# GpSimd sums the squares of tiles 0 to 3 of each norm, and a norm's first unit takes its high-part products first

## What is computed

```python
def rmsnorm(x, gain):
    xf = x.astype(jnp.float32)
    y = xf * lax.rsqrt(jnp.mean(xf * xf, axis=-1, keepdims=True) + EPS)
    return (y * gain.astype(jnp.float32)).astype(x.dtype)
...
        h = rmsnorm(x, norm1_g[i]) * (1.0 + sc1) + sh1
...
        x = x + g1 * y
        h = rmsnorm(x, norm2_g[i]) * (1.0 + sc2) + sh2
        x = x + g2 * swiglu(h, w_gate[i], w_up[i], w_down[i])
```

## Time and profile before

| | us |
|---|---|
| median of 3 runs (lowest to highest) | 1093.34 (1092.65 to 1093.69) |
| the profiled execution | 1092.77 |
| its span | 1091.0 |

### The profile page before, as it was taken

How to read it: one execution, slowest core, us unless ns; L and a number is a source line. 1 busy time by engine, 2 the same in 40 slices (tenths; PEclk the granted TensorE clock), 3 DMA queues, 4 the chain that set the end, 5 groups by cost and what they waited for, 6 DMA issues and landing times.

```text
span 1091.0 us, 19815 instructions
## 1 busy us (share of the span) xinstructions
PE 1020.5 (94%) x7643; PEld 968.2 (89%) x7643; DVE 784.0 (72%) x1108; ACT 505.5 (46%) x773; POOL 12.8 (1%) x27
## 2 busy tenths in 40 slices
PE   4699889999999989999999999998998999999997
PEld 4696568999999988977899999998887989999997
DVE  5876884898769867675489876986774579876432
ACT  3435743544442354535454443234866553443433
POOL 3000000000000000000000000001000000000000
PEclk9996759999999979999999999997999889999998
DMA  9980458499748948263249974887502429974500
GB/s 303 353 305 4 154 195 268 143 362 317 273 166 318 342 150 319 78 232 117 78 139 362 316 274 163 318 318 255 190 1 77 157 79 355 359 248 157 200 29 39
DMA packets 144413, 232.18 MB, mean 213 GB/s; under 512 B 6249, under 2 KB 75409, under 8 KB 144353
## 3 DMA queue, kind: packets, MB, share of 16 engines
q1 hardware_dynamic: 142993, 228.75, 60.8%
q0 software_dynamic: 1072, 2.05, 0.8%
q10 hardware_dynamic: 288, 0.54, 0.2%
HBM read 230.27 MB, written 1.05 MB: 212 GB/s over the span
## 4 chain that ended last, share of the span: by engine, by line
PE 82%; DVE 7%; ACT 4%; issue 3%; DMA 2%; SPq 1%; DVEq 0%; ACTq 0%
PE M L1425 22%; PE M L1426 22%; PE M L1427 22%; PE AUX L1914 3%; PE AUX L1535 3%; DVE ACC L936 2%; DMA RAW<-in_ada_w 1%; DVE WL L913 1%; ACT WH L565 1%; DMA RAW<-in_wqkv_a 1%; PE AUX L1758 1%; PE AUX L1543 1%; PE M L1702 1%; DVE TMP L993 1%; PE M L1701 1%
## 5 line engine op out<-in xcount | busy, mean ns | idle before, releaser
L1425 PE MATMUL M<-XH,WH 128*128 128x256 f32 x1520 | 441.5, 290 | 13.1 <-DVE XL L998 11.9
L1426 PE MATMUL M<-XL,WH 128*128 128x256 f32 x1520 | 436.2, 287 | 0.0
L1427 PE MATMUL M<-XH,WL 128*128 128x256 f32 x1520 | 435.7, 287 | 0.0
L913 DVE TENSOR_TENSOR WL<-RAW,WH 128x2048 fp32r<-128x2048 f32 x136 | 308.4, 2286 | 84.1 <-ACT WH L565 84.0
L565 ACT ACTIVATE WH<-RAW 128x2048 fp32r<-128x2048 f32 x136 | 258.6, 1914 | 230.4 <-PE M L1427 155.9
L1425 PEld LDWEIGHTS M<-XH,WH 128*128 128x128 f32 x1520 | 298.3, 196 | 16.4 <-issue 14.6
L1426 PEld LDWEIGHTS M<-XL,WH 128*128 128x128 f32 x1520 | 298.3, 196 | 0.2
L1427 PEld LDWEIGHTS M<-XH,WL 128*128 128x128 f32 x1520 | 297.9, 196 | 0.0
L936 DVE SCALAR_TENSOR_TENSOR ACC<-ADA,COND,ACC 128x512 f32<-128x512 f32 x266 | 199.9, 751 | 9.7 <-DMA ADA<-in_ada_w 0.6
L1425 PE MATMUL M<-MH,WH 128*128 (+1 forms) x528 | 150.6, 285 | 0.6 <-DVE TMP L1013 0.6
L1427 PE MATMUL M<-MH,WL 128*128 (+1 forms) x528 | 149.4, 283 | 0.0
(11 more groups left out here) (236 smaller groups left out, 971.4 us busy)
## 6 DMA issues: line engine op xcount, KB each, us to landing
ADA<-in_ada_w SPq DMA_DIRECT2D x68, 1024.0 KB, 6.4
RAW<-in_w_gate SPq DMA_DIRECT2D x44, 512.0 KB, 6.7
RAW<-in_w_up SPq DMA_DIRECT2D x44, 512.0 KB, 7.7
RAW<-in_w_down SPq DMA_DIRECT2D x44, 512.0 KB, 6.1
RAW<-in_w_ffn_in SPq DMA_DIRECT2D x44, 512.0 KB, 6.1
RAW<-in_wqkv_b SPq DMA_DIRECT2D x24, 512.0 KB, 6.2
RAW<-in_w_ffn_out SPq DMA_DIRECT2D x22, 512.0 KB, 4.3
RAW<-in_w_in SPq DMA_DIRECT2D x16, 512.0 KB, 5.7
```

Of the source, the lines that this page charges most:

```text
L913: dve.tensor_tensor(WL[:, s, :], RAW[:, s, :], WH[:, s, :], ALU.subtract).then_inc(l_ready, 1)
L1425: pe.matmul(out_ap, wh, xh, start=start, stop=False, skip_group_check=True)
L1426: pe.matmul(out_ap, wh, xl, start=False, stop=False, skip_group_check=True)
L1427: return pe.matmul(out_ap, wl, xh, start=False, stop=stop, skip_group_check=True)
```

## The change

- **Means.** There is a new tile SQS (128 x 256, fp32) and a new list on GpSimd, `square_sum(n)`: it adds the squares of tiles 0 and 1 into SQS, then tile 2, then tile 3, each as its square is ready, and counts `sq_sum`. Before it overwrites SQS it waits for the means of the norm before (`ssq_ready`). Norms 0 to 4 stand ahead of the seven loads for the mixer in GpSimd's list, norms 5 and 6 behind them.
- TensorE no longer takes the means of tiles 0 to 3: `early_means` and the places in the last `down_unit` go. After the last unit it takes those of tiles 4 and 5, waits for `sq_sum`, takes one of SQS, then those of tiles 6 and 7.
- **High parts first.** In the first unit after norms 1 to 5, TensorE waits for XH of an input tile, takes WH by XH and WL by XH for the four output tiles, then waits for XL of it and takes WH by XL. The products are the same. Norm 0's first unit has a loop of its own and stays.

```diff
+            def square_sum(n):
+
+                if n >= 1:
+                    pool.wait_ge(ssq_ready, n)
+                pool.wait_ge(sq_ready, KT * n + 2)
+                pool.tensor_tensor(SQS[:, :], TMP[:, 0, :], TMP[:, 1, :], ALU.add).then_inc(sq_sum, 1)
+                for j in range(2, 4):
+                    pool.wait_ge(sq_ready, KT * n + j + 1)
+                    pool.wait_ge(sq_sum, 3 * n + j - 1)
+                    pool.tensor_tensor(SQS[:, :], SQS[:, :], TMP[:, j, :], ALU.add).then_inc(sq_sum, 1)
+
+            for n in range(5):
+                square_sum(n)
             pool.wait_ge(w_used, U0["w_in"])
...
+            for n in range(5, 7):
+                square_sum(n)
...
+                if by_rows is not None and not last:
+                    for q, kt in enumerate(kts):
+                        xh, xl = x_of(kt)
+                        pe.wait_ge(hh_ready, KT * by_rows + kt + 1)
+                        for n, (tau, col) in enumerate(taus):
+                            cols = slice(q * width + col, q * width + col + P)
+                            pe.matmul(M[:, tau, :], WH[:, s, cols], xh, start=first and q == 0 and tau % 2 == 0, stop=False,
+                                      skip_group_check=True)
+                            pe.matmul(M[:, tau, :], WL[:, s, cols], xh, start=False, stop=False, skip_group_check=True)
+                        pe.wait_ge(xin_ready, KT * by_rows + kt + 1)
+                        for n, (tau, col) in enumerate(taus):
+                            cols = slice(q * width + col, q * width + col + P)
+                            mm = pe.matmul(M[:, tau, :], WH[:, s, cols], xl, start=False, stop=False, skip_group_check=True)
+                    mm.then_inc(w_used, 1)
+                    return
...
-                mm = token_means(AUX[:, 0, 0:2], TMP[:, j, :], ONES[:, 0:1], j == 0, j == KT - 1)
+                mm = token_means(AUX[:, 0, 0:2], TMP[:, j, :], ONES[:, 0:1], j == 4, j == KT - 1)
...
-            def norm(n, done=0, blocks=()):
-
-
-                for j in range(done, KT):
+            def norm(n, blocks=()):
+
+
+                for j in range(4, 6):
+                    mean_square(n, j)
+                pe.wait_ge(sq_sum, 3 * n + 3)
+                token_means(AUX[:, 0, 0:2], SQS, ONES[:, 0:1], False, False)
+                for j in range(6, KT):
                     mean_square(n, j)
...
-            group(U0["wo_a"], 1, 1, between=early_means(1))
+            group(U0["wo_a"], 1, 1)
...
-                down_unit(base, 10, hidden, range(8), None, False, True,
-                          between={4: [0], 5: [1], 6: [2, 3]}, norm_at=n)
+                down_unit(base, 10, hidden, range(8), None, False, True)
```

More of the change, by code:

```diff
@@ L216, in build @@
         RSTD = sb("RSTD", [P, 2])
+        SQS = sb("SQS", [P, T])
         IDB = sb("IDB", [P, P], BF16)
@@ L321, in build @@
         a_chain, acc_red, mod_ready, acc_turned, part_ready = (sem(n) for n in ("a_chain", "acc_red", "mod_ready", "acc_turned", "part_ready"))
-        x_ready, sq_ready, ssq_ready, std_ready = sem("x_ready"), sem("sq_ready"), sem("ssq_ready"), sem("std_ready")
+        x_ready, sq_ready, sq_sum, ssq_ready, std_ready = (sem(n) for n in ("x_ready", "sq_ready", "sq_sum", "ssq_ready", "std_ready"))
         rstd_ready, rstd_spread, coef_ready, t_ready = (sem(n) for n in ("rstd_ready", "rstd_spread", "coef_ready", "t_ready"))
@@ L1468, in group @@
                 unit(base, 2 * g + 1, i, taus, range(4, 8), operand, False, True, between=between)
-            def early_means(n):
-                return [lambda: mean_square(n, 0), lambda: [mean_square(n, 1), mean_square(n, 2)], lambda: mean_square(n, 3)]
             def values(base, k, kts, col, width, outs, first, last):
@@ L1549, in feed_forward @@
                 b0, steps = GU_BLOCKS[layer]
-                norm(2 * layer + 1, 4)
+                norm(2 * layer + 1)
                 group(base, 0, 0, 0, 3 * layer + 2)
@@ L1579, in feed_forward, with down_unit @@
                 fold_reduce(3 * layer + 1)
-                n = 2 * layer + 2
-                down_unit(base, 10, hidden, range(8), None, False, True,
-                          between={4: [0], 5: [1], 6: [2, 3]}, norm_at=n)
-            def down_unit(base, k, x_of, order, set0_free, first, ending, i=0, between=None, norm_at=None):
+                down_unit(base, 10, hidden, range(8), None, False, True)
+            def down_unit(base, k, x_of, order, set0_free, first, ending, i=0):
                 s = slot(base, k)
@@ L1600, in down_unit @@
                         mm.then_inc(bank_done, 1)
-                    for j in (between or {}).get(n, []):
-                        mean_square(norm_at, j)
             pe.wait_ge(const_in, 16)
@@ L1844, in project @@
                     value_rows(k, 1, kts, at // 2, at % 2, lower, not lower)
-            norm(2, 4)
+            norm(2)
             group(base, 0, 0, 0, 3)
@@ L1890, in _ @@
             unit(U0["wo_b"], 2, 0, last_rows[0], range(4, 8), heads, False, True, by_rows=4)
-            unit(U0["wo_b"], 3, 0, last_rows[1], range(4, 8), heads, False, True, between=early_means(3))
+            unit(U0["wo_b"], 3, 0, last_rows[1], range(4, 8), heads, False, True)
             feed_forward(1)
             base = U0["w_in"]
-            norm(4, 4)
+            norm(4)
             group(base, 0, 0, 0, 6)
@@ L1980, in _ @@
             unit(base, 2, 0, sets[0], range(0, 4), operand, False, True)
-            unit(base, 3, 0, sets[1], range(0, 4), operand, False, True, between=early_means(5))
+            unit(base, 3, 0, sets[1], range(0, 4), operand, False, True)
             feed_forward(2)
-            norm(6, 4)
+            norm(6)
             for m in range(2):
```

## The result

| | before | after |
|---|---|---|
| median of 9 runs each, on one chip (lowest to highest), us | 1095.03 (1092.65 to 1099.07) | 1085.59 (1084.05 to 1089.6) |
| the profiled execution | 1092.77 | 1084.05 |
| its span | 1091.0 | 1082.2 |

The ratio of after to before is 0.9918, with a 95% interval of 0.9897 to 0.9939: some 9 us faster, where 16 were forecast. The time lies above the range.

The account below looks back on a forecast made before the run. TensorE, 94% busy, bounds the kernel, losing time in waits at norm ends. 1.8 + 1.8 + 2 x (1.0 - 0.7) + 2 x 4.3 + 3.2 = 16.0 us off 1092.77: 1076.8, median 1077.3; range 1072 to 1084.

Parts of the forecast that it names:

- Norm 1, 1.8 us: Last unit before norm 1: without early means at 0.45 us each it ends 1.8 us sooner; the SQS mean costs nothing.
- Norm 6, 1.8 us: Norm 6: same chain as norm 1, with the same 0.75 us before the root, so 1.8 us gained.
- Norms 2 and 4, 4.3 us each: Norms 2 and 4: TensorE's 1.85 us stop goes, root at 388.0 instead of 392.34; 4.3 us each, bounds 3.0 to 4.8.
- High parts first, 0.65 us each: First units after norms 1 to 5: first product waits only for XH, 0.65 us earlier each, 3.2 us in all.
- Norms 3 and 5, 0.3 us each: Norms 3 and 5: 1.0 us gained each from fewer means, less 0.7 for GpSimd's add holding up VectorE's splits.
- rival 1: GpSimd and VectorE exclude each other, GpSimd winning each boundary in norms 0, 3, 5: 4.2 us less, 1081.5; chance 0.18.
- GpSimd's add, 0.7 us: Each GpSimd add of squares takes 0.7 us, chosen between 0.425 and 0.96; three adds take 2.1 us.
- Norm 0, nothing: Norm 0: means are done 13 us before the spread, which waits for VectorE's RSTD, so 0 us gained.
- Rival 2: Norms 2 and 4 stay at half clock through their means, GpSimd's add at 0.96: 2.7 us each, 1080.5; chance 0.14.
- Rival 3: Shorter gaps keep the full clock in some norms; two such norms give 3.2 us more: 1074.1; chance 0.13.
- Rivals 4 and 5: GpSimd's add becomes the bound, 1102 at 3 us (0.05); last unit's end isn't what norms wait for, 1091 (0.03).
- All three signs of being wrong: Profile after: splits over 2.24 us beside GpSimd, norm 2 SQS wait over 0.3, clock rise over 3.2 us after restart.

Follow-up runs that it names:

- high parts first alone: Kernel before with only the high-first order added, means left in their old place; 1091.53 us, ratio 0.9968.
- the stall alone: Kernel before, no GpSimd sums or high-first order: norms 2 and 4 take all eight means after the last unit; 1087.37 us, ratio 0.9927.
- the sums alone: Changed kernel with the first unit's old product order, keeping GpSimd's sums; 1086.05 us, ratio 0.9922.

## Why the prediction was right or wrong, point by point

- **Norm 1, 1.8 us: right.** From VectorE's add of tile 0 to the root it is 1.7 us shorter. It isn't seen at root 1, because that add comes at 171.75 us where it came at 169.38. This needn't be the change's doing. Two runs, high parts first alone and the stall alone, have the kernel before's program up to there, and in their profiles the add comes at 175.86 and 172.54; the profile before has it earliest of all thirteen. TensorE's time at half clock between root 0 and root 1 is 64.9 us after and 54.6 before, which may be the cause and isn't shown to be.
- **Norm 6, 1.8 us: right**, 1.84 with the little that high parts first gave in norm 5.
- **Norms 2 and 4, 4.3 us each: the term that was mis-sized.** It was 3.2. The mechanism held; I had "means 4 and 5 at full clock and the rest partly at half". The rest was wholly at half, and that is the whole error: with idle products and the same sum on GpSimd the clock stays up until 0.3 and 0.6 us before the roots, first add to root is 5.60 and 5.74 us, and the term is 4.4 and 4.2. SQS was late by 0.27 to 0.39 us in all these, behind adds that follow each other every 0.87 us and not every 0.7. 3.2 lies in my bounds of 3.0 to 4.8; the choice within them was the error, twice 1.1 us.
- **High parts first, 0.65 us each: the step that failed.** The first product is 0.65 us earlier as forecast. I assumed the clock "rises as long after the restart as now". It rises as long after the root, which I had priced (1.6 us for five), and from one profile to the next it moves by more than the 0.65 us. But even 1.6 was too high for norms 1, 3 and 5, because I carried all of each norm's gain to the end: "what follows each norm is dense TensorE work whose helpers start from the same norm". The helpers do start from the root, so a first product nearer to the root gains nothing on them: TensorE comes to the first product of unit 4 at most 0.2 us earlier, since it then waits for VectorE. The five give 1.0 us in this profile, not 3.2, and -0.5 to 1.7 in others.
- **Norms 3 and 5, 0.3 us each.** The exclusion, rival 1, is real, and in norm 3 it cost 1.05 us and in norm 5 0.55, where I took 0.7 each and the rival 1.4 and 0.7 on top of that. The page SBUF — State Buffer of the Trainium skill (Who interferes with whom) calls the ports that VectorE and GpSimd share an exclusive lock and says that issue order decides who blocks. Both traces of the changed kernel agree: an add of 0.74 us that starts 0.1 us ahead of a split makes it 0.5 us longer, and the next add ends 0.6 us after that split.
- **GpSimd's add, 0.7 us: right** where nothing interferes, 0.72 to 0.74, with 0.14 us between two that I didn't count. The estimate from the page GPSIMD Engine Reference of the Trainium skill (Elementwise — side-by-side cycle accounting), 0.83, was a little high.
- **Norm 0, nothing: right** to 0.25 us. Its adds take 1.02 and 1.85 us, four of VectorE's ada sums beside them 3.80 instead of 3.11, and the root is 0.75 us later. But the first split of weights (VectorE) starts at 39.26 instead of 39.02, and the two runs with norm 0 on TensorE have it at 39.24 and 39.05, so even the 0.24 is no more than spread.
- **The other rivals.** Rival 2 had 2.7 us for each of norms 2 and 4, at half clock with an add of 0.96: its clock came only for SQS and the last two tiles, its add did not, and 3.2 lies between it and the forecast. Rival 3, a fuller clock, came in none of the norms, until idle products made it. Rivals 4 and 5 are out: the add is 0.7 us, and the sums alone give nearly everything.
- **The signs.** In norms 1 and 6 last product to root is 2.2 us as before. In norm 2 it is 5.5, not 4 to 5. All three signs of being wrong came: a split of 2.78 us beside GpSimd, a wait for SQS of over 0.3 us (in norm 4), and a clock that rises 3.8 us after the restart.

The sum with measured terms: 1.7 + 1.8 + 2 x 3.2 + 1.0, and -0.1 and 0.3 for norms 3 and 5, is 11.1 us; less the 2.4 us by which norm 1's first add came later, 8.7. That this is the difference of the two profiled executions is no proof, since the terms are differences between the same roots. So 4.9 of the 7.3 us that were missing are mis-sized steps. The 2.4 lie within what profiles of one program differ by at that place, and a part of the rest is luck of the profile too: with the clock of its second profile the stretch to root 3 alone would have come out 2.5 us worse.

## What to carry to other kernels

Taking a stall out of an engine is worth its price only up to the next limit, so follow both sides of it: a point that all helpers start from (here the root) is a reason to move that point, and none to start sooner behind it. Offload a reduction only if the engine relieved of it has other work at that moment; with TensorE otherwise idle, eight short means on it beat five with a sum on GpSimd here, and products that nobody reads beat idling. Take the same program's profile more than once before a difference of 2 us between two profiles is given a cause. Before GpSimd gets SBUF work, look for VectorE instructions with two SBUF inputs in the same microseconds.

## What the runs showed of the hardware

- TensorE's clock went to 1.2 GHz around every norm. In the kernel before it never waited for work for more than 1.92 us at a time in norms 1 to 5. Seven 128x128 fp32 products around a root brought the half clock there down from 6.8 to 10.2 us a norm to between 0 and 6.8. They kept norm 1 at 2.4 GHz in three of five profiles. With four more in norms 3 and 5 the profiled execution had no half clock in norms 1, 3 and 4, and 3.4 us of it in norms 2 and 5.
- The moment of the fall differs between executions of one kernel. Before a root it costs 0.8 us for two means (1.84 against 1.03), and root 2 to root 3 differed by 2.5 us between two profiles of the same kernel. How much of the 4 us by which runs spread comes from it isn't shown.
- GpSimd's add of 128 x 256 fp32 takes 0.72 to 0.74 us alone; two of them take 5.3 us beside VectorE's splits. Beside VectorE's adds of X and a PSUM tile (norm 6) they stay at 0.73 to 0.74.
